# A two-layer hybrid encoder trunk on one core: splits of the gate loop last, a norm's spread inside the third chunk, first loads in halves, other branch banks, the last PLE turn in another order

## The reference

```python
def rmsnorm(x, g):
    xf = x.astype(jnp.float32)
    y = xf * lax.rsqrt(jnp.mean(xf * xf, axis=-1, keepdims=True) + EPS)
    return (y * g.astype(jnp.float32)).astype(x.dtype)

def swiglu(h, w_gate, w_up, w_down):
    return (jax.nn.silu(h @ w_gate) * (h @ w_up)) @ w_down
...
    merged = jax.nn.sigmoid(mga) * ya + jax.nn.sigmoid(mgb) * yb
    return merged @ w_out
...
    for i in range(DEPTH):
        x = x + 0.5 * swiglu(rmsnorm(x, norm_ff1[i]), ff1_w_gate[i], ff1_w_up[i], ff1_w_down[i])
        x = x + token_mixer(rmsnorm(x, norm_mix[i]), w_in[i], gla_gate_w2[i], gla_gate_b[i],
                            gla_norm[i], w_branch_a[i], w_branch_b[i], w_out[i])
        x = x + 0.5 * swiglu(rmsnorm(x, norm_ff2[i]), ff2_w_gate[i], ff2_w_up[i], ff2_w_down[i])
        g = jax.nn.sigmoid(rmsnorm(x, norm_ple[i]) @ ple_w_gate[i])
        x = x + g * (p[i] @ ple_w_proj[i])
    return rmsnorm(x, norm_final)
```

## Time and profile before

| | |
|---|---|
| median of three runs | 1224.85 us (1223.8 to 1227.88) |
| the profiled execution's own time | 1224.53 us |
| its span | 1222.7 us |
| PE busy | 97% of the span, 10226 matmuls |
| DVE, ACT, POOL busy | 68%, 49%, 12% |
| DMA | 218.77 MB, 179 GB/s |

### The profile page before, as it was taken

How to read it: one execution, slowest core, us unless ns; L and a number is a source line. 1 busy time by engine, 2 the same in 40 slices (tenths; PEclk the granted TensorE clock), 3 DMA queues, 4 the chain that set the end, 5 groups by cost and what they waited for, 6 DMA issues and landing times.

```text
span 1222.7 us, 23421 instructions
## 1 busy us (share of the span) xinstructions
PE 1190.4 (97%) x10226; PEld 1159.9 (95%) x10226; DVE 827.9 (68%) x919; ACT 593.7 (49%) x669; POOL 146.8 (12%) x137
## 2 busy tenths in 40 slices
PE   6999999999999999999999999999999999999997
PEld 6999999998889999999999999999888999999996
DVE  5766555688978666655767664548799777666545
ACT  6544434555555544444544444446456454444443
POOL 2000001002641100001210000100046120000011
PEclk9999999999999999999999999999999999999998
DMA  8655555454335565555456555554543456555540
GB/s 277 224 180 202 193 190 191 151 184 165 136 104 183 183 199 203 189 190 193 153 180 234 181 202 193 188 188 146 203 140 117 139 173 214 179 202 194 186 173 35
DMA packets 33734, 218.77 MB, mean 179 GB/s; under 512 B 5312, under 2 KB 5728, under 8 KB 7648
## 3 DMA queue, kind: packets, MB, share of 16 engines
q1 hardware_dynamic: 33056, 216.22, 51.7%
q10 hardware_dynamic: 576, 1.05, 0.3%
HBM read 216.21 MB, written 1.05 MB: 178 GB/s over the span
## 4 chain that ended last, share of the span: by engine, by line
PE 84%; DVE 6%; issue 3%; ACT 3%; POOL 2%; DMA 1%; POOLq 0%; SPq 0%; DVEq 0%; ACTq 0%
PE psum L361 27%; PE psum L363 27%; PE psum L362 27%; DVE w_lo L1115 2%; ACT w_hi L765 2%; POOL qlev L1075 1%; PE psum L605 1%; PE psum L483 1%; POOL klev L1074 1%; DMA x<-in_x 1%; PE psum L406 0%; PE psum L587 0%; PE psum L571 0%; DVE hB_lo L1442 0%; DVE hB_lo L1136 0%
## 5 line engine op out<-in xcount | busy, mean ns | idle before, releaser
L1115 DVE TENSOR_TENSOR w_lo<-raw,w_hi 128x2048 fp32r<-128x2048 f32 x201 | 468.5, 2334 | 221.1 <-ACT w_hi L765 221.1
L765 ACT ACTIVATE w_hi<-raw 128x2048 fp32r<-128x2048 f32 x201 | 385.4, 1917 | 428.0 <-PE psum L363 417.0
L361 PE MATMUL psum<-hA_hi,w_hi 128*128 128x256 f32 x1376 | 383.8, 279 | 0.0
L362 PE MATMUL psum<-hA_hi,w_lo 128*128 128x256 f32 x1376 | 380.1, 276 | 0.0
L363 PE MATMUL psum<-hA_lo,w_hi 128*128 128x256 f32 x1376 | 380.0, 276 | 0.0
L361 PEld LDWEIGHTS psum<-hA_hi,w_hi 128*128 128x128 f32 x1376 | 258.5, 188 | 3.4 <-issue 3.0
L362 PEld LDWEIGHTS psum<-hA_hi,w_lo 128*128 128x128 f32 x1376 | 258.5, 188 | 0.2
L363 PEld LDWEIGHTS psum<-hA_lo,w_hi 128*128 128x128 f32 x1376 | 258.3, 188 | 0.0
L361 PE MATMUL psum<-hB_hi,w_hi 128*128 128x256 f32 x832 | 232.5, 279 | 11.6 <-DVE w_lo L1514 8.4
L362 PE MATMUL psum<-hB_hi,w_lo 128*128 128x256 f32 x832 | 231.0, 278 | 0.0
L363 PE MATMUL psum<-hB_lo,w_hi 128*128 128x256 f32 x832 | 230.9, 277 | 0.0
(11 more groups left out here) (173 smaller groups left out, 1265.3 us busy)
## 6 DMA issues: line engine op xcount, KB each, us to landing
raw<-in_weights SPq DMA_DIRECT2D x203, 1024.0 KB, 4.9
raw<-in_weights ACTq DMA_DIRECT2D x4, 256.0 KB, 6.1
x<-in_x SPq DMA_DIRECT2D x4, 256.0 KB, 7.3
out<-gates SPq DMA_DIRECT2D x4, 256.0 KB, 2.4
relu<-in_p SPq DMA_DIRECT2D x2, 256.0 KB, 5.8
consts<-in_consts SPq DMA_DIRECT2D x1, 448.0 KB, 11.2
gnorm<-in_gla_norm SPq DMA_DIRECT2D x2, 64.0 KB, 5.0
consts<-in_consts SPq DMA_DIRECT2D x1, 64.0 KB, 10.7
```

Of the source, the lines that this page charges most:

```text
L361: pe.matmul(o, lh, rh, start=start, stop=False)
L362: pe.matmul(o, ll, rh, start=False, stop=False)
L765: act.activation(w_hi[:, s, :], raw[:, s, :], ACT.Copy).then_inc(hi_ready[s], 1)
L1115: dve.tensor_tensor(w_lo[:, s, :], raw[:, s, :], w_hi[:, s, :].bitcast(F32), ALU.subtract).then_inc(lo_ready[s], 1)
```

## The change

Seven edits, none of which adds or removes a matmul:

- In the gate loop both halves of the split of mg(j+3) go to the end of the turn's work: on ACT behind the decay and the attention's `Exp`, on DVE behind `distance`.
- `by_columns` can do one of a chunk's two columns, and `spread` goes between the two columns of q = 2. In the very first FFN `token_sums` goes there, and `spread` behind the second column; the squares of the first norm are put behind pieces of the splits.
- x and the first chunk are loaded in two halves each, all on SP's queue.
- The first branch starts with the k tiles of `oa2`, each column in a bank of its own, and waits for `oa3` only ahead of k = 2; banks are dealt anew.
- At the end of `WOUT` and of the layer DVE splits a chunk (two at the layer's end) ahead of `mean_square` instead of behind it.
- In the last PLE turn ACT's squares go behind the first tile's tanh, DVE's rest of tile 0 moves into tile 1's wait, and the split of the next layer's second chunk goes behind both tiles. In the last layer the final copies go behind both squares.
- `wi` is drained ahead of the split of MIX+7 on ACT.

```diff
-WOUT_BANKS = (6, 0, 2, 6)
+WOUT_BANKS = (6, 1, 4, 6)
...
-            for i in range(4):
-                sp.dma_start(x[:, 2 * i:2 * i + 2, :], a["x"][:, 2 * i:2 * i + 2, :]).then_inc(x_landed[i], 16)
+            for i in range(2):
+                sp.dma_start(x[:, 4 * i:4 * i + 4, :], a["x"][:, 4 * i:4 * i + 4, :]).then_inc(x_landed[i], 16)
                 if i == 0:
                     sp.dma_start(gains[:, 0, :], a["gains"][0, :, 0, :]).then_inc(gain_landed, 16)
+                half = slice(1024 * i, 1024 * i + 1024)
+                sp.dma_start(raw[:, 0, half], a["weights"][0, :, half]).then_inc(landed[0] if i else half_landed, 16)
...
+                    b = bank[UP_BANKS[(q - 2) % 6]]
+                    by_columns(s, b, h, (0,))
                     if q == 2:
+                        token_sums(L, k, 4) if first else spread(L, k, 4)
+                    by_columns(s, b, h, (1,)).then_inc(chunk_done[s], 1)
+                    if q == 2 and first:
                         spread(L, k, 4)
-                    by_columns(s, bank[UP_BANKS[(q - 2) % 6]], h)
...
+                def first_branch():
+
+                    s = operands(L, BRA)
+                    wh, wl = (w[:, s, :].rearrange("p (k n) -> p k n", n=512) for w in (w_hi, w_lo))
+                    wait_free(pe, L, "ya0")
+                    wait_drained(pe, L, "mg7")
+                    for k in range(4):
+                        if k % 2 == 0:
+                            wait_drained(pe, L, "oa3" if k else "oa2")
...
                     take(L, f"iq{i}", flat(iqT[:, 2 * i:2 * i + 2, :]))
-                    split(L, MIX + 6 + i)
+                    if i == 0:
+                        split(L, MIX + 6)
...
+                split(L, MIX + 7)
...
                     chunk_products(L, MGA + j)
                     if j == 7:
                         take_prob(7)
-                    split(L, MGA + j + 3)
...
                     if 0 < j < 7:
                         exps(j + 1)
+                    split(L, MGA + j + 3)
...
-                    take_pair(L, 4, i, None if last else hB)
+                    take_pair(L, 4, i, None if last else hB, i < 2)
...
+                    if c == 0:
+                        squares(L, 4, 2)
...
-                    split(L, MGA + j + 3)
                     if 0 < j < 7:
                         normalise(j + 1)
...
                         distance(4 << j, (2 << j) - 1)
+                    split(L, MGA + j + 3)
...
-                mean_square(L, 2, 4)
                 split(L, WOUT + 6)
+                mean_square(L, 2, 4)
...
-                    ins.then_inc(h_ready, 1)
+                    rest_tile(1).then_inc(h_ready, 1)
+                if not last:
+                    split(L, PGATE + 5)
+                    split(L, PGATE + 6)
                 mean_square(L, 4, 4)
```

More of the change, by code:

```diff
@@ L202, in hybrid_trunk @@
         gain_landed = sem("gain_landed")
-        x_landed = [sem(f"x_landed{i}") for i in range(4)]
+        x_landed = [sem(f"x_landed{i}") for i in range(2)]
         layer_landed = sem("layer_landed")
@@ L411, in ffn @@
                 k = 2 * f
+                first = L == 0 and f == 0
                 s = operands(L, off) if f else turn(L, off)[0]
@@ L421, in ffn @@
                 mm.then_inc(chunk_done[s], 1)
-                s = turn(L, off + 1)[0] if L == 0 and f == 0 else operands(L, off + 1)
+                s = turn(L, off + 1)[0] if first else operands(L, off + 1)
                 for m in range(4):
-                    if m == 2:
+                    if m == 2 and not first:
                         token_sums(L, k, 4)
-                    if L == 0 and f == 0:
+                    if first:
                         if m < 3:
@@ L675, in branch @@
                         mm.then_inc(chunk_done[s], 1)
-                wait_drained(pe, L, "oa3")
-                branch(BRA, "ya", oa_hi, oa_lo, 0, 0)
+                def first_branch():
[6 more added lines that the diff above has]
+                            wait_drained(pe, L, "oa3" if k else "oa2")
+                        for cc in range(2):
+                            cs = slice(cc * P, (cc + 1) * P)
+                            mm = three(bank[BANK_OF["ya0"] + cc][:, 0:T], wh[:, k, cs], wl[:, k, cs],
+                                       oa_hi[:, k, :], oa_lo[:, k, :], k == 0, k == 3)
+                    done(mm, "ya0")
+                first_branch()
                 branch(BRA, "ya", oa_hi, oa_lo, 0, 1)
@@ L984, in embed @@
                                        ).then_inc(h_hi_ready if c else tile_hi, 1)
-                if not last:
-                    act.wait_ge(sq_added, of_norm(L, 4, 3) + START)
-                    act.activation(squared[:, :, :], x[:, 6:8, :], ACT.Square).then_inc(sq_done, 1)
+                if last:
+                    for c in range(2):
+                        act.activation(final[:, 6 + c, :], x[:, 6 + c, :], ACT.Copy, scale=gains[:, 4, 6 + c:7 + c]).then_inc(final_scaled, 1)
+                else:
+                    squares(L, 4, 3)
                     split(L, PGATE + 6)
-            for i in range(4):
-                act.dma_start(raw[:, 0, piece(i)], a["weights"][0, :, piece(i)]).then_inc(piece_landed[i] if i < 3 else landed[0], 16)
             start_counts(act, drained)
@@ L1469, in embed, with rest_tile @@
                         split_pieces(L, n + 3)
-                    elif n + 3 < CHUNKS or not last:
+                    elif n + 3 < CHUNKS:
                         split(L, n + 3)
+                def rest_tile(c):
+                    dve.wait_ge(h_hi_ready if c else tile_hi, of_norm(L, 4, 4) if c else (L + 1))
+                    return dve.scalar_tensor_tensor(out=hB[1][:, 6 + c, :], in0=x[:, 6 + c, :], scalar=gains[:, 4, 6 + c:7 + c],
+                                                    in1=hB[0][:, 6 + c, :].bitcast(F32), op0=ALU.mult, op1=ALU.subtract)
                 for c in range(2):
@@ L1487, in embed @@
                 if not last:
-                    for c in range(2):
-                        dve.wait_ge(h_hi_ready if c else tile_hi, of_norm(L, 4, 4) if c else (L + 1))
-                        ins = dve.scalar_tensor_tensor(out=hB[1][:, 6 + c, :], in0=x[:, 6 + c, :], scalar=gains[:, 4, 6 + c:7 + c],
-                                                       in1=hB[0][:, 6 + c, :].bitcast(F32), op0=ALU.mult, op1=ALU.subtract)
-                    ins.then_inc(h_ready, 1)
+                    rest_tile(1).then_inc(h_ready, 1)
+                if not last:
+                    split(L, PGATE + 5)
+                    split(L, PGATE + 6)
                 mean_square(L, 4, 4)
-                if not last:
-                    split(L, PGATE + 6)
             start_counts(dve, lo_ready)
```

53 lines of the change are left out of this document (27 added, 26 removed).

## The result

The changed kernel took 1208.22 us (median of four runs, 1207.03 to 1209.19) against 1224.32 us for the kernel before (four runs, 1223.59 to 1227.88): a ratio of 0.9867, 95% interval 0.9854 to 0.9879. It is 16.1 us faster; 17.8 had been forecast. The profiled execution took 1208.47 us, its span is 1206.7 us.

A forecast was written before the change was run, and what follows sets the result against it. PE, busy 97% of the span, was taken as the bound, so only its waits and clock falls could be gained. Seven terms sum to 17.8 us off 1224.53, 1206.7, stated as 1207.0; range 1203 to 1212.5.

The forecast's parts named there:

- Gate loop, 9.2: Gate loop: six `qlev` waits and two falls of the clock go, 9.8 us together, 0.6 kept back for DVE's lag.
- The slack of 2.9 us: Gate loop, turn 1: with the splits last, POOL's pair ends at 302.1 and PE's chunk at 305.0, where a wait was.
- Spread, 2.0: Third chunk of the second FFNs: two PE waits for DVE's `w_lo` ahead of `spread` go, 2.0 us with short counting.
- `wi`, 1.1: `wi` drained ahead of a split: both PE waits go, 0.8 us and 0.3 for short counting.
- ya0, 2.3: First branch: 12 matmuls on `oa2` take 1.36 us and hide the rest of `oa3`; 2.3 us over two layers.
- end, 0.3: Kernel's end: a copy of 0.49 us leaves the way of the second tanh, gaining 0.3 us.
- The start, 1.0: Start: first matmul unchanged, within -0.5 and +1.5; later waits go, but q = 3 and q = 4 lose; 1.0 of 1.9 us.
- the start is worse: Rival at the start: first matmul waits for the whole 1 MB, 1.5 us later; 1210 us; chance 8%.
- The seam, 1.9: Between the layers: `h_ready` and q = 3 come 1.8 us earlier; gain 1.9 of 2.9 us, bounds 0.9 and 2.9.
- DVE becomes the bound of the loop: Rival in the gate loop: DVE's 8.4 us a turn exceeds PE's 7.9 and its lag surfaces; 1213 to 1216; chance 15%.
- More comes back than I count: Rival: gains land with less delay, first matmul 0.5 us earlier, two seams return 1.0 each; 1204 us; chance 15%.
- Weights late in the loop: Rival in the gate loop: ACT's and DVE's waits close a ring, PE waits for `w_lo` in some 12 turns; 1257; chance 1%.

The follow-up runs named there:

- e3: The changed kernel with only ACT's split of the gate loop back at the head of the turn, DVE's left last: 1208.12 us, ratio 0.9856.
- e4: The changed kernel with only DVE's split of the gate loop back behind the masks, ACT's left last: 1228.87 us, ratio 1.0035.
- e6: The changed kernel with DVE's `mean_square` of the second FFN's norm back ahead of its split of the third chunk: 1209.25 us, ratio 0.9881.
- e5: The changed kernel with PE's `spread` back at the head of the third chunk, in all FFNs but layer 0's first: 1208.32 us, ratio 0.9867.
- e7: The changed kernel with the first branch waiting for `oa3` ahead of its first product, new banks kept: 1210.27 us, ratio 0.9885.
- e2: The changed kernel with both splits of the gate loop, ACT's and DVE's, back in their old places: 1217.57 us, ratio 0.9936.
- e8: The changed kernel with SP issuing each layer's q = 3 chunk ahead of its wait for `h_ready` and the small loads: 1207.78 us, ratio 0.9863.
- e1: The changed kernel with the old start loads, x and first weights in quarters on two queues: 1206.75 us, ratio 0.9850.
- e12: The changed kernel with x and first weights loaded as a first quarter, then the other three quarters, on one queue: 1208.79 us, ratio 0.9868.
- e13: The changed kernel with quarter-first start loads, q = 3 issued ahead of the layers' small loads, and the first FFN's splits moved ahead: 1207.03 us, ratio 0.9854.
- e11: The changed kernel with the halves of the first weights issued by ACT on its own queue: 1207.60 us, ratio 0.9858.

## Why the prediction was right, and where it was off

The time fell within the range, and five of the seven terms came within 0.3 us. Of the signs named beforehand nearly all came: no `qlev` entry, a clock of 1.00 in both loops, mg7 5 us earlier, no `spread` entries for `w_lo`, SP's loads 1.8 us sooner, and no `w_lo` wait in the loops. One sign of being wrong came too, a first matmul behind 9 (10.00). The entry of L408 for `diag` is the final norm's, as in the kernel before.

- **Gate loop, 9.2.** Measured 9.5. mg7 begins 46.8 us after mg1 (47 forecast, 51.8 before), `klev` took 1.39 and `qlev` 1.30 us (medians of twelve), the granted clock stayed at 1.00. The size was right; the 0.6 kept back for DVE's lag was not needed. The step "With the splits last, ACT begins the decay when the chunk is done" is true and was not what gained, though: e3 has ACT's split first, its `klev` starts as late in turn 1 as before, and nothing is lost; e4 has it last with DVE's first and is 20.6 us above the change. What counts is DVE's place. The slack of 2.9 us was real (2.8), and e3 spends 1.9 of it.
- **Spread, 2.0; `wi`, 1.1; ya0, 2.3; end, 0.3.** Measured 2.2, 1.3, 2.2, 0.3. The terms of `wi` and the end were not taken back one by one; their waits are gone or shorter in the list. e6 and e5 show that it was the `mean_square` on DVE, as the prediction said, and e7 that it was the 12 matmuls.
- **The start, 1.0.** This is the larger mis-sized term: -0.8. The step that failed is "that gives a landing of w near 6.5 ... So 0, within -0.5 and +1.5": in the traced execution fifteen of sixteen parts had landed by 6.92 and the last at 8.53, and a load is there when its last part is. A duration of a load in steady state does not tell how late that part is at the start. The first matmul came 1.56 us later, just outside the term's own bound of 1.5 and where the rival *the start is worse* begins; of the waits behind it, those at q = 1 and at the diagonal went as forecast (2.2 us), and q = 3 and q = 4 lost 0.65 and 0.62 to DVE's order, as forecast (0.5 each).
- **The seam, 1.9.** Measured 1.2. SP's loads moved by the 1.8 us forecast, q = 1's wait is 0.67 (0.6 forecast). The step that failed is "q = 3 arrives 1.8 earlier": that chunk's hi part starts up to 1.6 us earlier or later against SP's first load from one execution to the next. Where it is in time the seam gains 1.7, near the term. The 0.3 at the token sums, from POOL's slowed additions, was not in it. The kernel before has one trace, so how much its own q = 3 moves is not known.
- **Rivals.** *DVE becomes the bound of the loop*: DVE is busy for 93% of the loop (60.5 of 65 us), its lag of 3 us was covered. *More comes back than I count* adds up to 1204.5 by its own terms, not 1204, which changes nothing. The rule of the Trainium skill that was weighed there (SBUF — State Buffer, "SBUF: two separate sides") was not put to the test for `distance`: it took 683 to 692 ns all 14 times, since POOL stood idle each time. `normalise` does meet POOL: one of its instructions took from 0.28 up to 1.38 us. *Weights late in the loop* is the closest to what e4 does, with one difference: PE waited not for the weights but for what was queued behind them.

How sure is a microsecond here? In the eight traced executions with halves on one queue whose start is otherwise that of the change (the change, e2 to e8), the first matmul stands between 9.30 and 10.74, and the slow spacing ends 2.9 to 6.1 us behind it, after 13 to 28 matmuls. With 0.1 us a matmul that alone is 1.5 us. q = 4 begins at 35.5 to 37.6, mean 36.3; the profiled execution of the change (36.89) is one of the later. The one trace of the kernel before has 36.21, also behind a long slow phase (26 matmuls), so the start's term is better told as "about 0, within 1" than as -0.8. The three fast executions of e1 have no trace and leave open that the old loads would have kept some 1.5 us. Why the slow phase differs so much between executions of the same instructions stays open.

## What to carry to other kernels

Ask of a piece of work that nobody waits for yet which instruction behind it, on its own engine, somebody does wait for, and which instruction beside it, on another engine, it slows. If the work is a chain over two engines, move its last link first: DVE's lo part alone gave the whole gain (e3), while ACT's hi part alone (e4) left DVE standing at a wait with wanted work behind it and turned a gain of 16 us into a loss of some 4. A split that meets a POOL instruction slows it, and can be slowed itself (two splits took 5.02 us beside POOL's additions), so look which POOL instruction runs at the new place too. Don't price a start by its first matmul: price it by the point from which nothing depends on it any more (here q = 4), since in e12 and e13 the gain of an early matmul that then starved was given back in full.

## What the runs showed of the hardware

- The first 512 KB of weights, issued third on one queue, were complete 2.1 to 3.5 us behind their median part in nine executions; the same load on a second queue 1.0 behind, in one (e11). DMA: Bandwidth & Descriptors of the Trainium skill, "Issuing engines are not separate DMA queues", says that a second issuing engine saves only the time to issue. The traces agree in the whole (first matmul 9.55 against 9.30 to 10.74). They add that the order of completion changes: x and gains were complete at 6.9 with two queues and at 4.65 with one, the first weights at 6.7 and 8.5.
- The first matmuls run at a spacing of 0.213 us instead of 0.113 while the column of the granted clock reads 1.00; 0.213 is also the spacing in e1 where the column reads 0.50. With a stop of 2.8 us in this phase it lasted until 17.8 (e12; 18.7 in e13), without one until 12.2 to 16.3 in eight executions.
- Between the start and the final norm the granted clock fell to 0.50 in four of fourteen traces, for 3.4 us (once 6.8): twice in the kernel before, once in e1, three times in e2, four times in e4. Each came within a wait of PE of 1.16 to 2.7 us or at most 2.1 us behind its end. Not every such wait was followed by one: the kernel before has waits of 1.16 and 1.28 us without.
- POOL's last two additions of 128x256 ahead of layer 1 take 0.74 us alone and 2.7 beside DVE's splits, the same in all thirteen executions that have them there (2.71 or 2.72, and 2.66).
- A POOL product of 128x512 took 1.3 us alone, 1.5 where it began 0.34 us ahead of the end of a DVE split, 1.9 where it began 0.75 ahead, and 3.44 where it began with one. The split that it met took 2.28 us, no longer than alone; a split that began behind it took up to 3.4 us.
